# One pair instead of two by owner products, and the first tile's expert rows added by TensorE

## Chip, cores, metric

The kernel runs on one core of one Trainium2 chip. The time is device microseconds of one execution, and the median of several runs is what is compared. Engines: TensorE (PE; PEld is its weight load), VectorE (DVE), ScalarE (ACT), GpSimd (POOL), SyncE (SP); a small q behind a name (SPq) is that engine's own sequencer, which issues transfers.

## What is computed

One encoder layer on x (512 tokens, 1024 columns, float32): a token mixer (windowed attention beside gated linear attention) is added to x, then a mixture of experts, then a last RMS norm. The change touches only what comes after the mixer:

```python
def hier_moe(x, ...):          # top-1 group of 4, then top-2 of the group's 8 experts
    ...
    for gi in range(N_GROUPS):
        h = jax.nn.silu(jnp.einsum('td,edf->tef', xt, w_gate[gi])) * jnp.einsum('td,edf->tef', xt, w_up[gi])
        out = out + jnp.einsum('tef,efd->td', h * combine[:, gi, :, None], w_down[gi])
...
    x = x + hier_moe(hn, ...)
return rms_norm(x, norm_final)
```

There are 32 experts of width 256, and each token goes to two of them. The weights of all experts are 100.7 MB (32 x 3 x 1.05 MB), read once.

## The kernel before

**Pairs.** The experts are worked through two at a time, 16 pairs. A pair has 128 slots, 64 of each of its experts. For pair n the kernel gathers the normed rows of its tokens from DRAM (`gather`, an indirect transfer by GpSimd, 128 x 1024), turns them (`turn_x`: 8 transposes, and copies of the two halves to `xgT` by ScalarE and VectorE), multiplies by the gate and the up weights (`gate_or_up`: 32 products of 256 columns each), takes silu and the product (`h_silu`, `h_sb`), turns the result (`turn_h`, `hT`), and multiplies by the down weights (`down`: 16 products of 512 columns). ScalarE and VectorE scale the two halves of the result by the slot's weight into one buffer `y`, and `scatter` writes its rows to `z_dram` (`expert_rows`). That array has two rows for each token, one for each of its two experts, and was zeroed early.

**Weights.** Each pair has six parts of 1 MB: gate, up and down of two experts. SyncE loads them into a ring of 23 places in the order `order`, each as soon as what lay there is used (`used`). Up to pair 12 the order is up n, gate n+1, down n; for pairs 13 and 14 it is up, down, and then the next gate. TensorE's program has the same order: gate n+1 stands ahead of down n as long as n+1 < LAST.

**The last two pairs.** `LAST` is 14: the loop with gathers, `y` and scatters does pairs 0 to 13. Behind it stands a block `If` for experts with more than 64 tokens, which is skipped with these inputs, and then pairs 14 and 15 are done in another way. Their down result is kept in two float32r parts, high (`ylast[i][0]`, ScalarE) and low (`ylast[i][1]`, VectorE), and TensorE multiplies them by `owner`, a matrix of ones that says which token owns which slot (`to_tokens`, two products of 512 columns a call). This adds the pair's result to the four tiles of 128 tokens without DRAM. A pair takes eight calls (four tiles, two halves of the columns). Pair 15's rows are gathered into a buffer of its own, `xg_last`.

**Where the tiles are summed.** The residual `x2` of tiles 0 and 1 is in SBUF, that of tile 3 in PSUM as `last_rows` (banks 6, 7), and ScalarE copies that of tile 2 to PSUM as `mid_rows` (banks 4, 5) when the last down result has left it (`mid_in`). So for tiles 2 and 3 TensorE adds in place; for tiles 0 and 1 it fills banks 0 to 3 and VectorE adds them to `x2` (`accumulate`, each signalled by `comb_done`, answered by `f_acc`).

**The scattered rows.** When the scatters of pairs 0 to 13 have landed, GpSimd signals `moe_done`, and SyncE loads the 2 MB x 2 of `z_dram` in four transfers of 1 MB (`zt`, one for each tile), with the gain `gfin` of the last norm between the third and the fourth. Tile 0's rows are added by VectorE (`add_row`, twice). Those of tiles 1 to 3 are added by TensorE: `rows_to_tokens` multiplies by `two_rows`, which sums each token's two rows, two float32 products of 512 columns a call, one call for each half of the columns.

**The finish.** For each tile ScalarE sums the squares and forms the mean, GpSimd takes the power -0.5, VectorE scales by it and the gain (tile 3 in two halves), and SyncE stores.

TensorE's order behind the loop, from line 1357 on: turn x of 14, gate and up 14, turn x of 15, turn h of 14, down 14, three calls of `to_tokens`, gate and up 15, three calls, turn h of 15, two calls, down 15, then the last eight calls of `to_tokens` among which stand the two calls of `rows_to_tokens` for tile 1, and at the end those for tile 2 and tile 3.

## Time and profile before

| | us |
|---|---|
| median of 3 runs | 604.86 (603.69 to 605.69) |
| the profiled execution, its time | 605.26 |
| its span, first to last instruction | 603.5 |
| TensorE busy | 577.0 (96% of the span) |
| VectorE, ScalarE, GpSimd busy | 260.3, 215.0, 60.3 |
| mean granted TensorE clock | 0.999 of full speed |
| moved by DMA | 155.78 MB, mean 258 GB/s |

Busy times are shares of the whole span, and this span has stages with different limits; the chain of waits says for each stretch which engine or transfer released the next step, and the windows what each engine did in it. A DMA's "to landing" counts from the start of its issue.

### The profile page before, as it was taken

The page shows a single profiled execution, that of the slowest core. Times are in us where ns is not written, and L with a number is a line of the kernel's source. Part 1 is how long each engine was busy: PE and PEld are TensorE (multiplying, and loading weights), DVE is VectorE, ACT ScalarE, POOL GpSimd, SP SyncE. Part 2 cuts the span into 40 slices and gives each one's busy share as a digit, 9 for nine tenths or more (in the row PEclk, how much of TensorE's full clock was granted, in tenths as well). Part 3 has the DMA queues.
Part 4 walks back from the last instruction along what each step waited for, and adds up shares of the span by engine and source line. Part 5 has one row for each costly group of instructions (what it writes and reads, how often), then busy time and mean ns, then how long its engine had stood idle before and what let it go on. Part 6 is the DMA issues. An engine that isn't in the chain of part 4 may idle for free.

```text
span 603.5 us, 8714 instructions
## 1 busy us (share of the span) xinstructions
PE 577.0 (96%) x3442; PEld 437.3 (72%) x3445; DVE 260.3 (43%) x584; ACT 215.0 (36%) x437; POOL 60.3 (10%) x104
## 2 busy tenths in 40 slices
PE   7999999999999999999999998999999999887795
PEld 4978989888788888888888874766666666543452
DVE  4646677645445765533472375212111211103255
ACT  6634566555786522422152241011111111111114
POOL 3110000001000001100000012012211121112001
PEclk9999999999999999999999999999999999999999
DMA  8365130712231222197789677999999999999995
GB/s 296 92 205 177 59 111 5 287 62 71 71 104 46 61 70 71 38 344 280 287 315 406 248 259 273 389 414 423 424 421 423 424 427 419 424 425 424 424 421 208
DMA packets 59291, 155.78 MB, mean 258 GB/s; under 512 B 8284, under 2 KB 38388, under 8 KB 47600
## 3 DMA queue, kind: packets, MB, share of 16 engines
q1 hardware_dynamic: 54512, 145.74, 63.2%
q0 software_dynamic: 4720, 9.45, 4.1%
q8 instruction: 28, 0.46, 0.3%
q14 instruction: 15, 0.12, 0.1%
q10 hardware_dynamic: 16, 0.00, 0.0%
HBM read 147.31 MB, written 15.75 MB: 270 GB/s over the span
## 4 chain that ended last, share of the span: by engine, by line
PE 79%; DMA 11%; DVE 3%; SPq 3%; ACT 1%; issue 1%; POOL 1%; DVEq 0%; POOLq 0%; ACTq 0%
PE mid_rows L810 17%; PE last_rows L810 16%; PE bank L1247 12%; DMA slot2b<-expert_w_up 9%; PE bank L810 7%; PE bank L803 5%; PE mid_rows L1267 5%; SPq L554 3%; PE bank L1321 2%; PE mid_rows L945 2%; PE last_rows L868 2%; PE mid_rows L1340 1%; DMA w<-w_in 1%; PE bank L1347 1%; PE mid_rows L868 1%; PE bank L923 1%
## 5 line engine op out<-in xcount | busy, mean ns | idle before, releaser
L1247 PE MATMUL bank<-slots,xgT 128*64 128x256 f32 x544 | 73.0, 381 | 4.5 <-DMA slot2b<-expert_w_up 1.9
L1910 DVE TENSOR_TENSOR w_low<-w,w_high 128x1024 fp32r<-128x1024 f32 x32 | 39.2, 1225 | 78.6 <-ACT w_high L1524 78.6
L1247 PEld LDWEIGHTS bank<-slots,xgT 128*64 128x64 f32 x544 | 49.2, 137 | 22.2 <-issue 4.0
L1524 ACT ACTIVATE w_high<-w 128x1024 fp32r<-128x1024 f32 x32 | 33.7, 1054 | 48.6 <-PE last_rows L810 48.6
L2265 DVE TENSOR_SCALAR y<-mid_rows,slot_weights 128x512 f32<-128x512 f32 x14 | 10.5, 751 | 88.4 <-PE mid_rows L1267 88.4
L1699 ACT ACTIVATE y<-mid_rows,slot_weights 128x512 f32<-128x512 f32 x14 | 9.6, 687 | 84.5 <-PE mid_rows L1267 56.4
L1247 PE MATMUL bank<-slot2b,xgT 128*64 128x256 f32 x208 | 32.9, 381 | 0.0
L1267 PE MATMUL mid_rows<-slots,hT 128*64 128x512 f32 x112 | 29.1, 594 | 2.7 <-issue 2.7
L1693 ACT ACTIVATE h_silu<-bank 128x256 f32<-128x256 f32 x14 | 5.4, 384 | 66.3 <-PE bank L1247 66.3
L810 PE MATMUL mid_rows<-x_high,w_high 128*128 128x512 f32 x72 | 28.7, 399 | 0.0
L810 PE MATMUL mid_rows<-x_high,w_low 128*128 128x512 f32 x72 | 28.2, 391 | 0.0
L810 PE MATMUL mid_rows<-x_low,w_high 128*128 128x512 f32 x72 | 28.1, 390 | 0.0
L2255 DVE TENSOR_TENSOR h_sb<-h_silu,bank 128x256 f32<-128x256 f32 x14 | 5.9, 422 | 48.7 <-ACT h_silu L1693 48.7
L1880 DVE CUSTOM_DVE_ANT_0 s_sb<-bank,bias,sink 128x256 f32<-128x256 f32 (+1 forms) x32 | 17.6, 549 | 19.4 <-PE bank L924 19.3
L810 PE MATMUL last_rows<-x_high,w_high 128*128 128x512 f32 x64 | 25.6, 400 | 0.0
L1247 PEld LDWEIGHTS bank<-slot2b,xgT 128*64 128x64 f32 x208 | 21.5, 137 | 5.2 <-issue 1.6
L810 PE MATMUL last_rows<-x_high,w_low 128*128 128x512 f32 x64 | 25.0, 390 | 0.0
L810 PE MATMUL last_rows<-x_low,w_high 128*128 128x512 f32 x64 | 24.9, 390 | 0.0
L1267 PEld LDWEIGHTS mid_rows<-slots,hT 128*64 128x64 f32 x112 | 10.2, 137 | 14.8 <-issue 14.4
L803 PEld LDWEIGHTS bank<-fixed,xg 128*128 128x128 f32 x120 | 14.6, 195 | 7.5 <-issue 5.8
L1503 ACT ACTIVATE softmax<-sink,softmax 128x1 f32<-128x1 f32 x32 | 9.3, 292 | 27.8 <-issue 16.3
L803 PE MATMUL bank<-fixed,xg 128*128 128x128 f32 x120 | 17.4, 288 | 1.2 <-DMA xg<-hn_rows,gtab 1.2
(430 smaller groups left out, 1391.5 us busy)
## 6 DMA issues: line engine op xcount, KB each, us to landing
slots<-expert_w_up SPq DMA_DIRECT2D x18, 1024.0 KB, 23.9
slots<-expert_w_gate SPq DMA_DIRECT2D x17, 1024.0 KB, 12.4
slots<-expert_w_down SPq DMA_DIRECT2D x15, 1024.0 KB, 23.9
slot2b<-expert_w_gate SPq DMA_DIRECT2D x9, 1024.0 KB, 16.9
w<-w_in SPq DMA_DIRECT2D x16, 512.0 KB, 3.6
slot2b<-expert_w_up SPq DMA_DIRECT2D x8, 1024.0 KB, 27.5
slot2a<-expert_w_down SPq DMA_DIRECT2D x6, 1024.0 KB, 21.4
w<-w_in SPq DMA_DIRECT2D x7, 840.0 KB, 4.5
```

The source lines that it names most:

```text
L554: sp.dma_start(ring[q % R], (g_rows, u_rows, d_rows)[m][:, 2 * pair + e, :]).then_inc(m_in[pair % 4][m], 16)
L803: return nc.tensor.transpose(out_, in_, K["ident"][0:n, 0:n])
L810: ins_ = mm(out_, stat[a_], mov[b_], start=first and q_ == 0, stop=last and q_ == 2)
L868: ins = mm(bank[5 + t % 2][:, 0:GW], x_[:, c, t * P:(t + 1) * P], job_view(w_, 0)[:, c, :], start=(h == 0 and q_ == 0 and c == 0), stop=(h ...
L945: ins = mm(bank[4][kv * DH:(kv + 1) * DH, :], tok[:, j, V_AT + kv * DH:V_AT + (kv + 1) * DH], pT[:, kv, k, :], start=(k == 0), stop=(k == ...
L1247: ins = mm(bank[2][e * SLOTS:(e + 1) * SLOTS, m * FE:(m + 1) * FE], xgT[:, c, e * SLOTS:(e + 1) * SLOTS], weights(own, m, e, c * FE, (c + ...
L1267: ins = mm(bank[4 + f][e * SLOTS:(e + 1) * SLOTS, :], hT[:, j, e * SLOTS:(e + 1) * SLOTS], down_rows(own, e, j, f), start=(j == 0), stop=( ...
L1321: ins = mm(bank[2][e * SLOTS:(e + 1) * SLOTS, m * FE:(m + 1) * FE], xgT[:, c, e * SLOTS:(e + 1) * SLOTS], weights(own, m, e, c * FE, (c + ...
L1524: A(wh2[:, u % 2, :], raw2[:, u % 2, :], ACT.Copy).then_inc(s["hi_done"], 1)
L1880: V.tensor_tensor_reduce(s_sb[:, i % 2, 0:n], bank[i % 2][:, 0:n], bias[:, h, band], 1.0, sink[:, h:h + 1], ALU.add, ALU.max, mx[:, i % 2: ...
L1910: V.tensor_tensor(wl2[:, u % 2, :], raw2[:, u % 2, :], wh2[:, u % 2, :].bitcast(F32), ALU.subtract).then_inc(s["lo_done"], 1)
L2265: V.tensor_scalar(y_sb[:, 512:1024], bank[5][:, :], weight, None, ALU.mult).then_inc(s["y_outD"], 1)
```

## The change

- `LAST` becomes 15. Pair 14 goes through the general loop: evaluated into `y`, scattered to `z_dram`, its owner matrix and its eight calls of `to_tokens` gone. Gate 14 moves ahead of down 13, in TensorE's program and in the order of the loads. Pair 15's rows are gathered into the common buffer `xg_in` after the turn of pair 14, and the buffer `xg_last` with its memset and wait is gone; so turn x of pair 15 comes behind down 14.
- SyncE waits for the scatters itself (by `scattered0` and `scattered1`), after `moe_done`, which GpSimd now gives when the last scatter is issued. The gain is loaded ahead of the four `zt` transfers, when down 14 is done. All four have the same layout.
- Tile 0's rows are added by two calls of `rows_to_tokens`, and `add_row` is gone. TensorE's order behind the last down: `to_tokens` for tiles 0, 1, 3 of both halves, rows of tile 0, rows of tile 1, `to_tokens` for tile 2, rows of tile 2, rows of tile 3.
- Tile 3's squares are taken in two halves, each scaled beforehand by the root of 1/1024, the second not before the last product; GpSimd adds the second sum to the first before the power.

The diff, without the parts that only drop the index of the pair:

```diff
-LAST = PAIRS - 2
+LAST = PAIRS - 1
...
-        xg_in, xg_extra, xg_last = (place_at(a_, n_, D)[:, :] for a_, n_ in
-                                    ((XL + D, "xg"), (MG, "xg_extra"), (YA + WSLOT + (NT - 1) * 2 * D, "xg_last")))
+        assert all(arrived[PAIRS - 3, m_] == 128 for m_ in range(3)) and (PAIRS - 3) % 4 == 1
+        xg_in, xg_extra = (place_at(a_, n_, D)[:, :] for a_, n_ in ((XL + D, "xg"), (MG, "xg_extra")))
...
-        ylast = [[place_at(MG + (2 * i_ + j_) * D, f"ylast{i_}{j_}", D, F32R)[:, :] for j_ in range(2)] for i_ in range(2)]
+        ylast = [place_at(MG + j_ * D, f"ylast{j_}", D, F32R)[:, :] for j_ in range(2)]
...
-        owner = v3(place_at(spare, "owner", 2 * SEQ, F32R), SEQ)
-        two_rows = place_at(spare + 2 * SEQ, "two_rows", P // 2)[:, :]
...
+        owner = place_at(spare, "owner", SEQ, F32R)
+        two_rows = place_at(spare + SEQ, "two_rows", P // 2)[:, :]
...
-                if later >= LAST - 1 and (m, e) == (2, 0):
+                if later >= LAST - 2 and (m, e) == (2, 0):
                     used(2, later - 4)
...
+            used(2, LAST - 1)
+            sp.dma_start(gfin, norm_final.partition_broadcast(P)).then_inc(s["gain_in"], 16)
             sp.wait_ge(s["moe_done"], 1)
+            for k in range(2):
+                sp.wait_ge(s[f"scattered{k}"], 16 * ((LAST + 1 - k) // 2))
             for t in range(NT):
                 rows = z_dram[2 * P * t:2 * P * (t + 1), :]
-                if t == NT - 1:
-                    sp.wait_ge(s["lx_done"], 4)
-                    sp.dma_start(gfin, norm_final.partition_broadcast(P)).then_inc(s["gain_in"], 16)
-                sp.dma_start(zt[:, t], rows.rearrange("(p w) n -> p w n", w=2) if t == 0 else
-                             rows.rearrange("(i p) n -> p i n", i=2)).then_inc(s[f"rows_in{t}"], 16)
+                sp.dma_start(zt[:, t], rows.rearrange("(i p) n -> p i n", i=2)).then_inc(s[f"rows_in{t}"], 16)
...
             for n in range(LAST):
-                if n + 2 < PAIRS - 1:
+                if n + 2 < PAIRS:
                     gather(n + 2, n + 2, n % 2, True)
-                else:
-                    pool.wait_ge(s["dn_done"], 2 * (LAST - 1))
-                    nc.gpsimd.memset(xg_last, 0.0).then_inc(s["zeroed"], 1)
-                    pool.wait_ge(s["zeroed"], 9)
-                    gather(PAIRS - 1, PAIRS - 1, 1, False, xg_last)
                 scatter(n, n, n % 2)
-
-            for k in range(2):
-                pool.wait_ge(s[f"scattered{k}"], 16 * (LAST // 2))
...
                 pool.wait_ge(s["ssA_done"], 2 * NT + t + 1)
+                if t == NT - 1:
+                    pool.wait_ge(s["ssA_done"], 3 * NT + 1)
+                    nc.gpsimd.tensor_tensor(rstd3[:, t:t + 1], rstd3[:, t:t + 1], ss2[:, t:t + 1], ALU.add).then_inc(s["last_mean"], 1)
+                    pool.wait_ge(s["last_mean"], 1)
                 nc.gpsimd.tensor_tensor(rstd3[:, t:t + 1], rstd3[:, t:t + 1], half[:, 0:1], ALU.pow).then_inc(s["rstd_done"], 1)
...
-            def to_tokens(i, f, tt, at, first):
-                pe.wait_ge(s["ly_lo"], 2 * i + f + 1)
+            def to_tokens(f, tt, at, first):
+                pe.wait_ge(s["ly_lo"], f + 1)
                 for q_ in range(2):
-                    ins = mm(bank[at][:, :], owner[:, i, tt * P:(tt + 1) * P],
-                             ylast[i][q_][:, f * 512:(f + 1) * 512], start=(first and q_ == 0), stop=(q_ == 1), skip_group_check=True)
+                    ins = mm(bank[at][:, :], owner[:, tt * P:(tt + 1) * P],
+                             ylast[q_][:, f * 512:(f + 1) * 512], start=(first and q_ == 0), stop=(q_ == 1), skip_group_check=True)
                 return ins
...
-            last_turn(0)
-            last_gate_up(0, 0)
-            last_gate_up(0, 1)
-            last_turn(1)
-            last_turn_h(0)
-            last_down(0)
-            pe.wait_ge(s["ltab_done"], NT)
-            to_tokens(0, 0, 0, 0, True).then_inc(s["comb_done"], 1)
-            to_tokens(0, 0, 1, 1, True).then_inc(s["comb_done"], 1)
-            to_tokens(0, 0, 3, 6, False)
-            last_gate_up(1, 0)
-            last_gate_up(1, 1)
-            pe.wait_ge(s["f_acc"], 1)
-            to_tokens(0, 0, 2, 0, True).then_inc(s["comb_done"], 1)
-            pe.wait_ge(s["f_acc"], 2)
-            to_tokens(0, 1, 0, 1, True).then_inc(s["comb_done"], 1)
-            to_tokens(0, 1, 3, 7, False)
-            last_turn_h(1)
-            pe.wait_ge(s["f_acc"], 3)
-            to_tokens(0, 1, 1, 0, True).then_inc(s["comb_done"], 1)
-            pe.wait_ge(s["f_acc"], 4)
-            to_tokens(0, 1, 2, 1, True).then_inc(s["comb_done"], 1)
-            last_down(1)
-            pe.wait_ge(s["ltab_done"], 2 * NT + 1)
-            to_tokens(1, 0, 0, 2, True).then_inc(s["comb_done"], 1)
-            to_tokens(1, 0, 1, 3, True)
-            to_tokens(1, 0, 3, 6, False)
-            pe.wait_ge(s["mid_in"], 1)
-            to_tokens(1, 0, 2, 4, False)
+            last_turn()
+            last_gate_up(0)
+            last_gate_up(1)
+            last_turn_h()
+            last_down()
+            pe.wait_ge(s["ltab_done"], NT + 1)
+            to_tokens(0, 0, 2, True)
+            to_tokens(0, 1, 3, True)
+            to_tokens(0, 3, 6, False)
+            to_tokens(1, 0, 1, True)
+            to_tokens(1, 1, 0, True)
+            to_tokens(1, 3, 7, False)
+            pe.wait_ge(s["rows_in0"], 32)
+            rows_to_tokens(0, 0, 2).then_inc(s["comb_done"], 1)
+            rows_to_tokens(0, 1, 1).then_inc(s["comb_done"], 1)
             pe.wait_ge(s["rows_in1"], 32)
             rows_to_tokens(1, 0, 3).then_inc(s["comb_done"], 1)
-            pe.wait_ge(s["f_acc"], 6)
-            to_tokens(1, 1, 0, 1, True).then_inc(s["comb_done"], 1)
-            to_tokens(1, 1, 1, 0, True)
-            to_tokens(1, 1, 3, 7, False)
             rows_to_tokens(1, 1, 0).then_inc(s["comb_done"], 1)
-            pe.wait_ge(s["mid_in"], 2)
-            to_tokens(1, 1, 2, 5, False)
+            for f in range(2):
+                pe.wait_ge(s["mid_in"], f + 1)
+                to_tokens(f, 2, 4 + f, False)
             for tt, banks in ((2, (4, 5)), (3, (6, 7))):
                 pe.wait_ge(s[f"rows_in{tt}"], 32)
                 for f in range(2):
...
-            for t in range(NT):
+            for t in range(NT - 1):
                 if t < 2:
-                    act.wait_ge(s["f_acc"], 9 + t)
+                    act.wait_ge(s["f_acc"], 2 * (t + 1))
                 else:
-                    act.wait_ge(s["comb_done"], (12, 14)[t - 2])
+                    act.wait_ge(s["comb_done"], 2 * (t + 1))
                 if t >= 1:
                     act.wait_ge(s["ssA_done"], 2 * NT + t)
                 act.wait_ge(s["act_step"], step(A(junk3[:, :], summed_rows(t), ACT.Square, accum_out=ss3[:, t:t + 1])))
                 A(rstd3[:, t:t + 1], ss3[:, t:t + 1], ACT.Copy, scale=1.0 / D, bias=EPS).then_inc(s["ssA_done"], 1)
+            t = NT - 1
+            act.wait_ge(s["ssA_done"], 2 * NT + t)
+            act.wait_ge(s["comb_done"], 2 * NT - 1)
+            act.wait_ge(s["act_step"], step(A(junk3[:, 0:512], last_rows[:, 0:512], ACT.Square, accum_out=ss3[:, t:t + 1], scale=ROOT)))
+            A(rstd3[:, t:t + 1], ss3[:, t:t + 1], ACT.Copy, bias=EPS).then_inc(s["ssA_done"], 1)
+            act.wait_ge(s["comb_done"], 2 * NT)
+            A(junk3[:, 512:D], last_rows[:, 512:D], ACT.Square, accum_out=ss2[:, t:t + 1], scale=ROOT).then_inc(s["ssA_done"], 1)
...
-            def add_row(i):
-                return step(V.tensor_tensor(x2[:, 0, :], x2[:, 0, :], zt[:, 0, i, :], ALU.add))
...
-            dve.wait_ge(s["rows_in0"], 32)
-            dve.wait_ge(s["f_acc"], 6)
-            first_row = add_row(0)
-            last_low(1, 0)
-            dve.wait_ge(s["dve_step"], first_row)
-            second_row = add_row(1)
-            last_low(1, 1)
-            dve.wait_ge(s["dve_step"], second_row)
-            accumulate(7, 0, 0, 2)
-            accumulate(8, 1, 0, 3)
-            accumulate(9, 0, 1, 1)
-            accumulate(10, 1, 1, 0)
+            last_low(0)
+            last_low(1)
+            accumulate(1, 0, 0, 2)
+            accumulate(2, 0, 1, 1)
+            accumulate(3, 1, 0, 3)
+            accumulate(4, 1, 1, 0)
```

## Rows read from the trace of the kernel before

**Rows 1.** Page, slices of the span (GB/s in each 40th) and GpSimd's DMA queue.
```profile
GB/s 296 92 205 177 59 111 5 287 62 71 71 104 46 61 70 71 38 344 280 287 315 406 248 259 273 389 414 423 424 421 423 424 427 419 424 425 424 424 421 208
...
q0 software_dynamic: 4720, 9.45, 4.1%
```

**Rows 2.** Chain of waits, 555 to 604 us: start, us, what.
```profile
532.32 30.16 DMA slot2b<-expert_w_up
...
562.62 3.67 PE bank L1321 x32
...
583.80 3.58 PE mid_rows L1340 x16
...
589.44 1.01 PE bank L1353 x4
...
593.71 1.89 PE mid_rows L1353 x8
```

**Rows 3.** Windows: length, then PE, PEld, DVE, ACT, POOL busy, PEclk, DMA, GB/s.
```profile
562.62:587.38 24.76, 24.00 (x157) 13.94 (x157) 9.49 (x16) 3.43 (x6) 0.00 (x0) 1.00 1.01 422
587.38:597.29 9.91, 9.91 (x41) 4.12 (x40) 6.79 (x8) 5.80 (x12) 1.37 (x3) 1.00 0.47 195
```

**Rows 4.** Line 745's scatters (all 14); line 664's loads, the last one alone.
```profile
L745 POOL DMA_INDIRECT expert_rows<-y,zcol x14: 1002/1011/1023, 395.3 to 555.9; - x14
...
DMA to landing us min/median/max: 7.8/8.1/9.0
...
L664 SPq DMA_DIRECT2D zt<-expert_rows x1: 4573/4573/4573, 570.8 to 570.8; - x1
...
DMA to landing us min/median/max: 22.4/22.4/22.4
```

**Rows 5.** Timeline of TensorE, 548.4 to 563 us: start, us, instruction, idle before.
```profile
549.43 0.50 PE L803 MATMUL bank<-fixed,h_sb 128*128 128x128 f32 x2 [0.94 <-DVE h_sb L2255]
550.45 3.65 PE L1267 MATMUL mid_rows<-slot2a,hT 128*64 128x512 f32 x16 [0.52 <-DVE hT L2259]
554.04 1.16 PE L803 MATMUL bank<-fixed,xg 128*128 128x128 f32 x8
556.03 4.33 PE L1321 MATMUL bank<-slot2b,xgT 128*64 128x256 f32 x32 [0.83 <-DVE xgT L2326]
```

**Rows 6.** Timeline of TensorE's weight loads within line 1321's first 32 products.
```profile
556.03 0.62 PEld L1321 LDWEIGHTS bank<-slot2b,xgT 128*64 128x64 f32 x7 [1.02 <-DVE xgT L2326]
557.18 2.72 PEld L1321 LDWEIGHTS bank<-slot2b,xgT 128*64 128x64 f32 x25 [0.52 <-issue]
```

**Rows 7.** Line 554: last loads of the up and of the down weights.
```profile
L554 SPq DMA_DIRECT2D slots<-expert_w_up x1: 2339/2339/2339, 552.2 to 552.2; - x1
...
DMA to landing us min/median/max: 24.9/24.9/24.9
...
L554 SPq DMA_DIRECT2D slots<-expert_w_down x1: 2264/2264/2264, 558.0 to 558.0; - x1
...
DMA to landing us min/median/max: 24.0/24.0/24.0
```

**Rows 8.** Timeline of ScalarE and GpSimd: a half copy, tile 2's squares, two one-column operations.
```profile
588.02 0.59 ACT L1755 ACTIVATE mid_rows<-x 128x512 f32<-128x512 f32 x1
...
595.62 1.03 ACT L1763 ACTIVATE squares<-mid_rows 128x1024 f32<-128x1024 f32 x1 [0.42 <-PE mid_rows L1353]
...
596.77 0.20 ACT L1764 ACTIVATE row_norms<-row_norms 128x1 f32<-128x1 f32 x1
...
5.63 0.19 POOL L685 TENSOR_SCALAR row_norms<-row_norms 128x1 f32<-128x1 f32 x1 [3.43 <-ACT squares L1414]
...
598.79 0.55 POOL L794 TENSOR_TENSOR row_norms<-row_norms,half 128x1 f32<-128x1 f32 x1 [1.20 <-ACT row_norms L1764]
```

**Rows 9.** Timeline of TensorE at the start: products of zeros.
```profile
1.80 2.74 PE L830 MATMUL last_rows<-nil_rows 128*128 128x512 bf16 x6 [1.80 <-POOL nil_rows L680]
...
8.24 1.03 PE L830 MATMUL last_rows<-nil_rows 128*128 128x512 bf16 x4
```

123 lines of the change are left out of this document (46 added, 77 removed).

## Prediction

> **What bounds the kernel now.** I read four views, in this order. The page's slices come first: DMA moves 421 to 425 GB/s from the 26th slice to the 39th, so from about 380 us almost to the end the transfers are saturated [rows 1]. The chain of waits then says where that stops mattering. The up weights of pair 14 are on their way for 30.16 us and land at 562.48; from there the chain is TensorE work: up of pair 14 at 562.62, the last down from 583.80, a call of `rows_to_tokens` for 1.01 (four records, two per float32 product), and two calls for tile 2 in 1.89 [rows 2]. So there is a front part that ends when bytes have landed, and a back part that TensorE sets. The windows split the back part in two: from the start of up 14 to the end of the last down, 562.62 to 587.38, TensorE is busy 24.00 of 24.76 us; from there to 597.29 it is busy all 9.91 us, with 40 weight loads, that is 0.248 us for each product [rows 3]. After 597.29 come squares on ScalarE, a power on GpSimd, the scaling on VectorE and the store, to 603.5.
>
> I therefore sum the change in four terms: when up 14 can start, how long from there to the end of the last down, how many products follow, and how long the finish is. All are against the profiled execution (605.26 us with a span of 603.5), which is 0.40 above the median of the runs, 604.86; I carry the difference over to the median.
>
> **Term 1, start of up 14.** The new order of loads swaps gate 14 and down 13 and moves no byte, so up 14 stays at the same place in the queue. TensorE now does gate 14 at once after the turn of pair 14 and down 13 behind it; both lie in the time in which it waits for the landing anyway: before, it had 2.26 us of idle ahead of up 14, and down 13 will only wait for its own weights there. One thing moves in the queue: the scatter of pair 13, issued at 555.90 before [rows 4], follows down 13, so it goes out after up 14's weights have landed or nearly. GpSimd's queue moved 9.45 MB [rows 1] in its 30 gathers and scatters, 0.3 MB each, or 0.7 us at 424 GB/s. Bounds: 0 and -0.7; I take **-0.3**, since some of it has not moved by 562.5 either way.
>
> **Term 2, up 14 to the end of the last down.** Removed from TensorE between them: eight calls of `to_tokens` for pair 14 (16 products at 0.248, 4.0 us). But they covered other things, which now stand bare. Three stalls, each priced by what pair 13 and the turn of pair 14 show [rows 5]: the end of up to the start of down is 548.49 (549.43 less its idle 0.94) to 550.45, 1.96 us, for silu, product, turn and copy, and it now comes twice; the end of down 13 at 554.10 to the start of the next gate at 556.03 is 1.93 us, for the turn of x and its two copies, which before was hidden for pair 15 under silu of pair 14. Then there is gate 14 itself, 4.33 us where an up of the same 32 products takes 3.67: within it the weight loads stopped for 0.52 at 557.18, with nothing in the profile to wait for [rows 6]. It is the first such block behind the skipped `If`; before, the DMA wait hid it, and now gate 15 is that block, so I charge it. The sum is 3.67 + 1.96 + 3.65 + 1.93 + 4.33 + 3.67 + 1.96 + 3.65 = 24.82, against 24.76 before: **0.0**. Without the stop it would be -0.7.
>
> The landings set a floor under this. The last up weights were issued at 552.2 and took 24.9 us (577.1), the last down weights at 558.0 and took 24.0 (582.0) [rows 7]; the scatters of pairs 13 and 14 now lie in front of the second, up to 0.7 us more. With terms 1 and 2 the last up wants its weights near 577.8 and the last down near 583.4, so both are just covered. The floor for the end of the last down is 582.0 + 3.65 = 585.7, or 586.4 with the scatter. My own is 587.1.
>
> **Term 3, products after the last down.** Before: eight calls of `to_tokens` (16 records) and six of `rows_to_tokens` (24), 9.91 us. After: again eight, but eight of `rows_to_tokens`, as tile 0's two are new, 48 records. Eight more at 0.248 are 2.0; by the 1.89 of tile 2's two calls it is 1.9. I take **+1.9**. What they replace are the two adds of rows on VectorE, which lay beside TensorE's work and were on no chain, so nothing is gained there. TensorE must pass every one of these products, in order, before tile 3 is complete. The wait for the low part of the second half of the columns costs nothing: it is ready about 1.5 us after down, and three calls cover that.
>
> **Term 4, the finish.** Tile 3's squares are halved: the first half runs while the last product call runs, the second behind it. But tile 2's squares come first: they begin when tile 2 is complete, 1.9 us before the end of TensorE, and take 595.62 to 596.97 with the copy of the mean, 1.35 us. A half of 512 columns from the 512-column copy (0.59) plus the read of the sum is about 0.7, its copy 0.2, then 0.7 again [rows 8]: ScalarE ends 1.1 us behind TensorE (before: 1.4). GpSimd gets an add ahead of its power. No row has this add of one column: the nearest are its multiply-add of one column, 0.19, and its power, 0.55 [rows 8]; I take 0.28 with the hand-over, as it is arithmetic like the first. Sum: -0.3 + 0.3 = **0.0**, bounds -0.4 and +0.5.
>
> **What is hidden.** The pair-14 evaluation into `y`, its scatter and the wait for it replace owner work: ScalarE and VectorE are idle there. The order of things for the rows is: down 14 ends near 571.9, y is written to 572.7, the scatter goes out at 573.6 and lands 7.8 to 9.0 us later [rows 4], at 581.4 to 582.6. SP, which has nothing else to do, issues the four loads then. Before, four loads and the gain landed by 593.2; the last load by itself took 22.4 us from its issue at 570.8, behind the weights [rows 4]. After, the queue still holds the last weights and the gain until about 584, so the loads follow without a hole and at 2.5 us each land at about 586.5, 589, 591.5 and 594. TensorE wants them at 590.2, 592.2, 595.3 and 597.2. The cover is 3 us; beyond it each us of lateness is one on the end. One rule of the Trainium skill bears on that cover: the page "DMA: Bandwidth & Descriptors", section "Anatomy of one DMA — SWDGE (gpsimd) path", gives a fixed cost of some 2 us beside the bytes; an estimate by it puts a load of 1 MB on an empty queue at 4.4 us, the first rows at 587, and changes no term.
>
> **Sum.** -0.3 + 0.0 + 1.9 + 0.0 = +1.6 us: 606.9 for the profiled execution, **606.5** for the median. By the low ends it is -1.0 (the floor 586.4) + 1.8 - 0.4 = +0.4, by the high ends 0 + 0.2 + 2.1 + 0.5 = +2.8.
>
> **Rivals.** (a) *The landing floor is reached.* The stop in gate 15 does not come and the last down starts as its weights land: 586.4, and with the cheap finish +0.4 us, 605.3. For it: the stop is seen once. (b) *The rows come late.* The scatter is now on the path of all four loads; if it lands over 3 us later than any in the trace, or the loads run at half their pace, tile 3's rows are last: +1 to +4 us more, 607.5 to 610.5. Against it: 14 scatters landed within 7.8 to 9.0. (c) *The clock falls.* TensorE now idles in one piece, down 13's end (559.5) to up 14, up to 3.0 us, where the longest shown is 2.26 at a granted clock of 1.00. At a lower level up 14 would go at the pace of the first products, 0.46 each against 0.26 of the same kind later [rows 9], by 1.77: 2.8 us on 3.67, so 609.3. The Trainium skill, page "TensorE: Matmul & The Clock Gate", section "HAM oscillation — how this bites in real kernels", states such a fall after a DMA wait between bursts; by that rule it would be 609.3 too, while the trace keeps its clock over every gap it has. (d) *Faster.* The 4.0 us of pair 14's products come off whole, because silu, turn and copies overlap with something: the last down ends at 583.4, the tail adds 1.9, -2.1 us, 602.8. It decides only if the last down weights have landed by 579.7; they landed at 582.0, and I see no bytes that leave the queue.
>
> **Chances.** Measurements of this kernel tell about 0.3% from no change, 1.8 us, and my sum lies just inside. The forecast 0.60, (a) 0.15, (b) 0.12, (c) 0.06, (d) with anything unseen 0.07. The forecast's own range is 605.6 to 607.7, and I put 0.4 of it beyond 606.7. Slower: 0.12 + 0.06 + 0.24 = 0.42; faster 0.07; the same 0.51. The range from 604.6 to 609.0 holds the forecast, (a) and most of (b), and leaves (d) and most of (c) out.
>
> **What would show it.** Up 14 starts at 562 to 562.6; the last down starts without a DMA wait, or with one if (a); from its end to the last product 11.8 us with 48 weight loads and no idle; all `zt` loads issued at 581 to 583 and landed by 595; a gap of 0.5 in the weight loads of gate 15; granted clock 1.00 throughout; ScalarE's last sum 1.1 us behind TensorE. It is wrong if the end of the last down is not within 586.3 to 587.6, or if TensorE waits for rows.

## The result, and the profile after

| | before | after |
|---|---|---|
| median of the runs taken together on one chip | 605.28 us (603.69 to 606.94, 20 runs) | 606.14 us (605.55 to 607.14, 20 runs) |
| the profiled execution, its time | 605.26 | 605.96 |
| its span | 603.5 | 604.2 |
| TensorE busy | 577.0 | 577.9 |
| moved by DMA | 155.78 MB | 156.02 MB |

The ratio is 1.0014 with an interval of 1.0007 to 1.002: the changed kernel is slower by about 0.9 us, and that is within the 0.3% (1.8 us) that the prediction counts as no change. In the profiled executions it is slower by 0.7.

Read first the page of the changed kernel: the engines' busy time, the row of GB/s in 40 slices, GpSimd's queue, and the shares of the chain.

```profile
PE 577.9 (96%) x3436; PEld 436.3 (72%) x3437; DVE 252.6 (42%) x570; ACT 214.5 (36%) x438; POOL 61.2 (10%) x106
...
GB/s 300 87 206 177 57 113 3 294 55 71 71 104 54 53 69 71 42 341 289 289 314 400 241 271 274 386 416 421 425 421 423 423 426 421 425 424 425 423 369 257
...
q0 software_dynamic: 4864, 9.69, 4.2%
...
PE 77%; DMA 11%; SPq 5%; DVE 3%; ACT 2%; issue 1%; POOL 1%; DVEq 0%; POOLq 0%; ACTq 0%
```

The queue is as saturated as before up to the 38th slice [rows 1]; then 369 and 257 stand where 421 and 208 stood, because the rows are now loaded at the very end. GpSimd's queue moved 0.24 MB more, the pair that is scattered now.

Then the chain of waits of the changed kernel, from 540 us on: start, length, what.

```profile
551.83 25.35 DMA slots<-expert_w_up
577.18 0.14 issue
577.31 3.69 PE bank L1320 x32
...
582.94 3.65 PE mid_rows L1338 x16
586.59 1.12 PE bank L1345 x4
...
589.84 3.58 PE bank L1351 x16
593.42 1.13 PE mid_rows L1345 x4
594.55 1.89 PE mid_rows L1351 x8
```

This differs from [rows 2] in one thing that matters. Before, the last transfer in the chain was the up weights of pair 14, landing at 562.48. Now it is the up weights of pair 15, landing at 577.18. In this chain all that TensorE does between them is off the path.

The windows of the changed kernel, cut at the same three events as [rows 3] (start of up 14, end of the last down, last product), with the finish as the third:

```profile
562.00:586.59 24.59, 20.43 (x141) 10.85 (x141) 5.67 (x15) 2.74 (x5) 2.17 (x3) 1.00 0.98 396
586.59:598.14 11.55, 11.54 (x49) 4.82 (x48) 6.08 (x7) 6.10 (x13) 1.84 (x3) 1.00 0.68 270
598.14:604.20 6.06, 0.00 (x0) 0.00 (x0) 2.69 (x3) 1.17 (x5) 1.04 (x3) 0.75 0.69 277
```

In the first, TensorE is busy 20.43 of 24.59 us, where it was busy 24.00 of 24.76: 3.6 us of work went and only 0.17 of time. In the second it is busy throughout, as before, with 48 weight loads instead of 40. The four terms of the prediction, against the profiled execution of before (span +0.7):

| term | forecast | measured | from |
|---|---|---|---|
| 1. start of up 14 | -0.3 | -0.62 | 562.62 to 562.00 |
| 2. up 14 to the end of the last down | 0.0 | -0.17 | 24.76 to 24.59 |
| 3. products behind it | +1.9 | +1.64 | 9.91 to 11.55 |
| 4. finish | 0.0 | -0.15 | 603.5 - 597.29 = 6.21, to 6.06 |
| sum | +1.6 | +0.70 | |

TensorE's timeline of the changed kernel shows where the stalls lie, and one thing that was not expected (below): start, length, instruction, idle before it.

```profile
556.28 5.35 PE L1266 MATMUL mid_rows<-slot2b,hT 128*64 128x512 f32 x16 [2.47 <-issue]
562.00 3.24 PE L1246 MATMUL bank<-slot2b,xgT 128*64 128x256 f32 x28 [0.37 <-DMA slot2b<-expert_w_up]
...
577.31 3.67 PE L1320 MATMUL bank<-slots,xgT 128*64 128x256 f32 x32 [0.41 <-DMA slots<-expert_w_up]
581.92 0.50 PE L802 MATMUL bank<-fixed,h_sb 128*128 128x128 f32 x2 [0.93 <-DVE h_sb L2307]
582.94 3.65 PE L1338 MATMUL mid_rows<-slots,hT 128*64 128x512 f32 x16 [0.52 <-DVE hT L2309]
```

The line 1266 row is down of pair 13. Its 16 products took 5.35 us; the last down takes 3.65, as it did before. The windows over it show why (the column behind the five busy times is the granted clock):

```profile
556.20:556.70 0.50, 0.42 (x2) 0.23 (x4) 0.00 (x0) 0.00 (x0) 0.00 (x0) 1.00 1.00 418
556.70:557.20 0.50, 0.50 (x4) 0.19 (x2) 0.00 (x0) 0.00 (x0) 0.00 (x0) 0.65 0.98 410
557.20:560.00 2.80, 2.80 (x8) 0.90 (x6) 0.00 (x0) 0.51 (x1) 0.00 (x0) 0.50 1.03 430
560.00:560.40 0.40, 0.40 (x4) 0.29 (x2) 0.00 (x0) 0.18 (x1) 0.16 (x1) 0.67 0.97 410
560.40:561.60 1.20, 1.20 (x6) 0.17 (x2) 0.00 (x0) 0.00 (x0) 0.02 (x1) 1.00 1.03 430
```

TensorE had idled 2.47 us (the view says "issue", but the last down weights of pair 13 landed only at 556.19), began at full clock, fell to 0.50 (the 1.2 GHz level) some 0.6 us later, and had it back at about 560.2. Down 13 ended at 561.63, and up 14 waited another 0.37 us for its weights: the fall was hidden, with that to spare.

Last, the four loads of the rows in the changed kernel:

```profile
L666 SPq DMA_DIRECT2D zt<-expert_rows x4: 377/466/1163, 580.8 to 582.9; - x4
...
DMA to landing us min/median/max: 5.7/8.8/11.6
```

They were issued at 580.77, 581.2, 582.4 and 582.9 and landed at 586.5, 589.3, 592.0 and 594.5; TensorE wanted them at 589.8, 591.6, 594.5 and 596.2. It waited for none, with 1.8 to 3.3 us to spare.

### The profile page after: what moved, and what is told of

It reads as the page before. It is cut to its first block, busy times and chain, and to the rows that moved or that the text cites. A ratio compares the mean times of both kernels' runs of the same rounds, so it can differ in the third digit from the quotient of the medians.

```text
span 604.2 us, 8686 instructions
## 1 busy us (share of the span) xinstructions
PE 577.9 (96%) x3436; PEld 436.3 (72%) x3437; DVE 252.6 (42%) x570; ACT 214.5 (36%) x438; POOL 61.2 (10%) x106
## 2 busy tenths in 40 slices
DMA packets 59563, 156.02 MB, mean 258 GB/s; under 512 B 8368, under 2 KB 38472, under 8 KB 48000
## 4 chain that ended last, share of the span: by engine, by line
PE 77%; DMA 11%; SPq 5%; DVE 3%; ACT 2%; issue 1%; POOL 1%; DVEq 0%; POOLq 0%; ACTq 0%
PE mid_rows L809 17%; PE last_rows L809 16%; PE bank L1246 12%; DMA slots<-expert_w_up 9%; PE bank L809 7%; PE bank L802 5%; SPq L555 5%; PE mid_rows L1266 5%; PE mid_rows L944 2%; PE last_rows L867 2%; DMA w<-w_in 1%; PE mid_rows L867 1%; PE bank L922 1%; PE bank L1117 1%; PE bank L923 1%
## 5 line engine op out<-in xcount | busy, mean ns | idle before, releaser
L1246 PE MATMUL bank<-slot2b,xgT 128*64 128x256 f32 x240 | 36.6, 381 | 0.4 <-DMA slot2b<-expert_w_up 0.4
L1246 PEld LDWEIGHTS bank<-slot2b,xgT 128*64 128x64 f32 x240 | 23.6, 137 | 7.5 <-DMA slot2b<-expert_w_up 1.2
## 6 DMA issues: line engine op xcount, KB each, us to landing
slots<-expert_w_down SPq DMA_DIRECT2D x15, 1024.0 KB, 24.8
```

What stands on the lines that cost most here:

```text
L1246: ins = mm(bank[2][e * SLOTS:(e + 1) * SLOTS, m * FE:(m + 1) * FE], xgT[:, c, e * SLOTS:(e + 1) * SLOTS], weights(own, m, e, c * FE, (c + ...
```

## The experiments

Eleven runs, ten of them of a kernel with something altered and one of the changed kernel again, in three batches, each timed against runs of the kernel before on the same chip. By the numbers in their names, the first batch is `e1`, `e2`, `e3` and `e5`, the second `e4`, `e8`, `e9` and `after_again`, the third `e6`, `e7` and `e11`. The medians of before were 605.63 (31 runs), 605.19 (24 runs) and 605.46 (24 runs); in the second batch the changed kernel was run again (`after_again`):

> The changed kernel itself, on the same chip as the three above, so that they can be set against it: 0.14% above the kernel before, by either theory. Its granted clock in down 13 shows whether the fall there comes each time.

Measured: 606.40 (11 runs), ratio 1.0021, interval 1.0012 to 1.003, which agrees with the first result; its down 13 took 5.35 us as well, and its up 14 started at 561.90. Medians of one kernel differ by up to 0.44 us between batches (605.19 to 605.63), so smaller differences are not read from times of different batches; there the ratios to the kernel before are compared. Where a rise or fall inside a kernel is told, it is from its profiled execution, and spans are compared (before 603.5, changed 604.2, changed again 604.1).

**Rows of tile 0 by TensorE, in the kernel before (`e2_before_rows0_tensor`).** The third term alone.

```diff
...
             to_tokens(1, 0, 0, 2, True)
+            pe.wait_ge(s["rows_in0"], 32)
+            rows_to_tokens(0, 0, 2).then_inc(s["comb_done"], 1)
...
             to_tokens(1, 1, 0, 1, True)
+            rows_to_tokens(0, 1, 1).then_inc(s["comb_done"], 1)
...
-            first_row = add_row(0)
...
-            second_row = add_row(1)
```

> The kernel before with only this part of the change: tile 0's rows are added by TensorE with two calls behind the last down, and not by VectorE. My theory: eight more product records on the path, +1.7 to +1.9 us, near 607.1. Rival (the calls hide in waits of the tail or run faster among others): under +0.8.

Measured: 607.38 (8 runs) against 605.63, ratio 1.0027, interval 1.0014 to 1.0039, span 605.5, +2.0. So the eight records do cost, and VectorE's two adds, now gone, give nothing that shows. The chain of waits of this kernel behind its last down shows the price of each call:

```profile
587.76 1.01 PE bank L1352 x4
588.77 0.67 PE bank L1346 x2
589.43 0.46 PE last_rows L1346 x2
...
595.83 1.89 PE mid_rows L1352 x8
```

A pair of products costs 0.46 where the same kind stands ahead of it and 0.67 right behind a call of `rows_to_tokens`. From the first product here (587.06) to the end of the last (597.53 + 1.89 = 599.42) it is 12.36 us, and by the same reading of before's trace it was 9.96: +2.4 for the eight records in before's order. In the changed kernel the rows of tiles 0 and 1 stand together, 16 records in 3.58 us or 0.224 each, and the term was +1.64. So the new order of calls gives back about 0.8 us of what the new products cost. Here the last down ended 0.3 earlier than in before's trace, so the span rose by 2.0 and not by 2.4.

**Rows of tile 0 by VectorE, in the changed kernel (`e1_rows0_vector`).** The reverse.

```diff
...
-            pe.wait_ge(s["rows_in0"], 32)
-            rows_to_tokens(0, 0, 2).then_inc(s["comb_done"], 1)
-            rows_to_tokens(0, 1, 1).then_inc(s["comb_done"], 1)
...
             last_low(0)
             last_low(1)
+            dve.wait_ge(s["rows_in0"], 32)
+            dve.wait_ge(s["dve_step"], add_row(0))
+            dve.wait_ge(s["dve_step"], add_row(1))
```

> The changed kernel with one part undone: tile 0's rows are added by VectorE again, here behind the two low parts (so from about 588.1), and TensorE has six calls for rows. My theory (the tail of products sets the end, 16 records of rows cost 3.58 us, half of that is tile 0's): the last product ends 1.8 us sooner, near 596.4, and the time is about 1.7 us under the changed kernel, near 604.4, which is also under the kernel before. Rival (VectorE becomes the bound: its two adds of 1.2 us delay tile 0's and tile 1's sums, and with them ScalarE's squares): less than 0.8 us gained.

Measured: 606.51 (12 runs, 605.03 to 607.22), ratio 1.0007, interval 0.9996 to 1.0018; the profiled execution was the fastest of them, with a span of 603.3. There the last down ended at 586.69, but TensorE came to tile 1's rows earlier and found them missing:

```profile
590.57 1.94 PE L1352 MATMUL bank<-zt,two_rows 128*64 128x512 f32 x8 [0.64 <-DMA zt<-expert_rows]
592.43 1.20 PE L1346 MATMUL mid_rows<-ylast,owner 128*128 128x512 f32 x4
593.57 1.94 PE L1352 MATMUL mid_rows<-zt,two_rows 128*64 128x512 f32 x8
```

Of the 1.8 us that leave TensorE (eight records at 0.224), 0.64 come back as that wait, and tile 3's rows landed at 595.50 for products that start at 595.54, 0.2 behind the pace of the ones ahead. The last product ends at 597.48, 0.66 sooner than in the changed kernel and not 1.7 as expected. By the spans it is 0.9 below the changed kernel; by the ratios 0.4, with intervals that overlap, so this run alone does not prove the price of the eight records.

**The rows held back (`e4_rows_held`).** To see where their cover ends, SyncE issues the loads only when the first half of the last down is done.

```diff
+            sp.wait_ge(s["ldn_done"], 1)
             for t in range(NT):
                 rows = z_dram[2 * P * t:2 * P * (t + 1), :]
```

> The changed kernel with the four loads of the rows held until the first half of the last down is done (near 584.9 instead of 580.8). By the landings of the changed kernel the rows had 3.3, 2.3, 2.5 and 1.8 us to spare for tiles 0 to 3. My theory (that spare is the cover, and the last landings follow the issue by as much as the queue is empty then): TensorE waits for rows and the time rises by 1 to 2.4 us. Rival (the loads are paced by other transfers ahead, so the hold costs nothing): the same within 0.3 us.

Measured: 607.39 (5 runs), ratio 1.0035, interval 1.0021 to 1.0048, so 1.0 above the changed kernel in the same batch (with only five runs, and intervals that overlap). The loads left at 584.9 to 586.3, that is 3.4 to 4.1 us later, and landed in 4.8 to 10.9. Waits on `zt` now stand ahead of tile 1's rows (0.51, 592.19), and tile 3's start at 597.28, 1.0 later than in the changed kernel. With 1.8 to 3.3 us of cover and 3.4 to 4.1 of delay, about one microsecond should show, and one did.

**Tile 3's squares whole again (`e3_whole_squares`).** The fourth term.

```diff
-            for t in range(NT - 1):
+            for t in range(NT):
...
-                if t == NT - 1:
-                    pool.wait_ge(s["ssA_done"], 3 * NT + 1)
-                    nc.gpsimd.tensor_tensor(rstd3[:, t:t + 1], rstd3[:, t:t + 1], ss2[:, t:t + 1], ALU.add).then_inc(s["last_mean"], 1)
-                    pool.wait_ge(s["last_mean"], 1)
...
```

> The changed kernel with tile 3's squares taken whole again and no add on GpSimd. By the two traces the way from the last product to tile 3's scaling took 2.21 us with halves and 2.08 whole, so my theory expects the same time within 0.2 us, rather a little less. Rival (the halves hide part of the squares and save 0.4 us or more): 0.4 to 0.6 us more than the changed kernel.

Measured: 606.65 (11 runs), ratio 1.0018, interval 1.0006 to 1.003, span 604.1. The changed kernel's ratio is 1.0014 to 1.0021: no difference that can be told, as the term's 0.0 said.

**Gate 14 behind down 13 again (`e8_old_order`).** TensorE's order and that of the loads as before.

```diff
-            turns += ([(n_, 1), (n_ + 1, 0), (n_, 2)] if n_ + 1 < LAST else
+            turns += ([(n_, 1), (n_ + 1, 0), (n_, 2)] if n_ + 1 < LAST - 1 else
...
-                if n + 1 < LAST:
+                if n + 1 < LAST - 1:
                     gate_or_up(n + 1, 0, *weights_of(n + 1))
...
                 down(n, *weights_of(n))
+                if n + 1 == LAST - 1:
+                    gate_or_up(n + 1, 0, *weights_of(n + 1))
```

> The changed kernel with down 13 ahead of gate 14 again, in TensorE's program and in the order of the loads. Theory A (the swap only moves work about in the time in which TensorE waits for up 14's weights): the same as the changed kernel within 0.3 us, up 14 between 561.8 and 562.5. Theory B (the swap itself brings the fall of the clock in down 13 and costs in the median): no fall between 550 and 562, and 0.4 us or more less.

Measured: 606.95 (8 runs), ratio 1.003, interval 1.0019 to 1.004; 0.55 above the changed kernel of the batch, with intervals that overlap. Timeline of its TensorE:

```profile
557.07 5.13 PE L1246 MATMUL bank<-slot2b,xgT 128*64 128x256 f32 x32 [2.49 <-DMA slot2b<-expert_w_gate]
563.37 1.51 PE L1246 MATMUL bank<-slot2b,xgT 128*64 128x256 f32 x11 [1.16 <-DMA slot2b<-expert_w_up]
```

Now gate 14 waits for its weights for 2.49 us and takes 5.13 us instead of 3.67, and up 14 starts 1.37 later than in the changed kernel, waiting for weights that are themselves late. Its scatter of pair 13 went out at 556.38, ahead of those weights' landing, against 563.42 in the changed kernel. By itself this fits the reason given for term 1; but 0.3 MB is 0.7 us at 424 GB/s and the start moved by 1.37, so the scatter is at most half of it. Part of the rest was there before the orders differ: the first load in another order is issued at 518.81, and the up weights that land at 525.53 and 528.00 in the changed kernel, issued long before, landed at 525.87 and 528.84 here. And `e2_before_rows0_tensor`, which has before's order and sends that scatter at 556.64, also ahead of the landing, starts up 14 at 561.78, earlier than the changed kernel. So executions of one order differ here by as much as the two orders do, and the scatter's share isn't shown.

**TensorE kept busy in the gap (`e5_kept_busy`).** Nine products of constants that nobody reads, between gate 14 and down 13 (eight of them are in the trace's records).

```diff
+                if n == LAST - 2:
+                    keep_busy(9)
                 down(n, *weights_of(n))
```

> The changed kernel with nine products of constants (bfloat16, 512 columns, into a free bank) between gate 14 and down 13, where TensorE idled 2.47 us before its clock was granted at 0.50 within down 13. Theory A (the fall is hidden in the wait for up 14's weights): down 13 takes 3.65 instead of 5.35 us, the granted clock stays at 1.00, up 14 still starts at 562.0 and the time is the same within 0.2 us. Theory B (in the median run the fall reaches up 14 or delays the scatter of pair 13 so that later steps are late): 0.3 to 0.8 us less.

Measured: 606.86 (12 runs: eight from 606.43 to 606.90, four from 608.41 to 608.64), ratio 1.0024, interval 1.0012 to 1.0036. Its timeline, and its windows over up 14 (which begins at 561.77):

```profile
553.60 1.89 PE L1117 MATMUL bank<-fixed,onesb 128*128 128x512 bf16 x8 [0.16 <-issue]
556.05 3.65 PE L1266 MATMUL mid_rows<-slot2b,hT 128*64 128x512 f32 x16 [0.56 <-issue]
561.77 1.08 PE L1246 MATMUL bank<-slot2b,xgT 128*64 128x256 f32 x8 [2.07 <-DMA slot2b<-expert_w_up]
```

```profile
562.60:563.00 0.40, 0.40 (x8) 0.26 (x6) 0.00 (x0) 0.00 (x0) 0.00 (x0) 1.00 1.07 451
563.00:566.00 3.00, 3.00 (x18) 1.76 (x16) 0.00 (x0) 0.00 (x0) 0.00 (x0) 0.51 1.01 425
566.00:566.60 0.60, 0.60 (x6) 0.31 (x4) 0.00 (x0) 0.00 (x0) 0.00 (x0) 0.61 0.97 403
```

Down 13 has its 3.65 back, and ends 2.07 us before the weights of up 14 land. Behind that gap the clock falls again, in up 14, which took 5.36 us instead of 3.67. Gate 15 started at 574.68, 1.46 later than in the changed kernel, and the last down at 583.77, 0.83 later. In this execution, filling a covered gap opened a bare one. The median rose too, but by the ratios only by 0.2 to 0.6 us over the changed kernel, with intervals that overlap. What puts four of the runs 1.6 us above the others isn't shown; each profile is one execution.

**Less to load (`e6_before_less_bytes`, `e7_less_bytes`).** Half the columns of the second up part of pair 13 are not loaded, 0.52 MB, in the kernel before and in the changed one. Half of one expert's up weights are left out of the computation.

```diff
+                if later == PAIRS - 3 and order[q][1:] == (1, 1):
+                    sp.dma_start(ring[q % R][:, 0:PART // 2], u_rows[:, 2 * later + 1, 0:PART // 2]).then_inc(m_in[later % 4][1], 16)
+                    continue
                 load_part(q)
```

> The kernel before, with half the columns of the second up part of pair 13 not loaded: 0.52 MB leave the queue ahead of the up weights of pair 14, 1.24 us at 424 GB/s. It leaves out half of one expert's up weights, so that expert's result is formed with what lay in the place. Theory (the front part ends when bytes have landed, the back part is TensorE's): up of pair 14 starts 1.2 us earlier, at 561.4, and all behind it too, so the time falls by 1.2 us, unless down 13 and gate 14 hold it at their own pace (end of gate 14 at 560.4, so not before that). Rival (the transfers are not what sets the front): no change of the median beyond 0.3 us.

> The changed kernel with the same half of the second up part of pair 13 not loaded (it leaves out half of one expert's up weights). Theory: up of pair 14 is allowed by its weights at 560.8 instead of 562.0, but down 13 with its clock fall (556.3 to 561.6) now ends behind that, so it starts at 561.6 to 561.7, only 0.4 us earlier; the last down's weights land 1.2 us earlier too and gate 15 to the last down keep their pace, so the median falls by 0.4 us, the 0.41 of waiting ahead of the last up goes as well: 0.4 to 0.8 us in all. Rival (the fall of the clock does not come, or is no limit): 1.2 us less, as for the kernel before.

Measured: the kernel before went to 603.60 (6 runs), ratio 0.9969, interval 0.9958 to 0.9981, span 601.8, -1.7. The changed one went to 605.37 (11 runs, 604.25 to 607.54), ratio 1.0004, interval 0.9991 to 1.0016, with 604.25 and a span of 602.5 in the profiled execution, -1.7 too. The kernel before moved by more than the 1.24 us of the bytes. The changed one did so in its profiled execution, which is the fastest of its eleven; by the ratios it fell by 0.6 to 1.0 us only, its runs spread over 3.3 us, and that is about what the theory (0.4 to 0.8) had put. The theory's mechanism, that down 13 with its fall of the clock would hold the start of up 14 back, is refuted by the profile all the same: down 13 itself started earlier, at 554.54, fell likewise (5.35 us), and up 14 began at 560.19, 1.81 sooner. The chains of waits of the two, first `e6_before_less_bytes`, then `e7_less_bytes`:

```profile
549.93 25.53 DMA slots<-expert_w_up
...
575.60 3.67 PE bank L1324 x32
```

```profile
549.97 25.48 DMA slots<-expert_w_up
...
575.58 3.69 PE bank L1323 x32
```

In both the last up starts 0.14 us behind the landing of its weights (575.46 and 575.45), and all behind it moved with that, 1.7 us. This is the answer to where the removed work went: the kernel before and the changed one have the same floor there. In before the last up started at 577.27 with the weights landed at 577.13 [rows 7]; its row in the timeline shows no idle,

```profile
577.27 3.67 PE L1321 MATMUL bank<-slots,xgT 128*64 128x256 f32 x32
```

and in the changed kernel it started at 577.31, with a landing of 577.18. The weight loads tell more than the products. First before's, then the changed kernel's first load of the last up:

```profile
577.24 0.88 PEld L1321 LDWEIGHTS bank<-slots,xgT 128*64 128x64 f32 x10 [0.35 <-issue]
```

```profile
577.28 0.84 PEld L1320 LDWEIGHTS bank<-slots,xgT 128*64 128x64 f32 x9 [0.84 <-issue]
```

Both come 0.10 to 0.11 us behind the landing, and the one of before behind a pause of 0.35 where the pauses inside a block are under 0.1. So before, too, started its last up on the landing: its loads waited some 0.3 us, while its products, still busy with the ones ahead, show no idle. After, the products idle 0.41 there. In `e2_before_rows0_tensor`, which has before's front, the last up waited 0.45 us for its weights. Of the eight calls of pair 14 three lay ahead of this landing, where nothing is gained, and five between the last up and the last down, where silu, product, turn and copy take 1.96 us without them. What was gained lies there: from the start of the last up to the end of the last down it took 10.11 us before (577.27 to 587.38) and 9.28 after (577.31 to 586.59).

Why 0.52 MB were worth 1.7 us and not 1.24 in the two profiles has a likely answer in them. The up weights that landed at 475.11 in before and at 475.12 in the changed kernel landed at 474.54 and 474.53 here, 40 us ahead of the issue of the shortened load. These two executions were thus 0.6 us early before the edit could act, and without that 1.1 is left in each, near the 1.24. What gave them the head start isn't shown.

The traces with before's front also bear on the stop of 0.52 in gate 14, which the prediction priced. In `e6_before_less_bytes` the weight loads of gate 14 stop for 0.15, in `e2_before_rows0_tensor` not at all:

```profile
557.19 2.73 PEld L1324 LDWEIGHTS bank<-slot2b,xgT 128*64 128x64 f32 x25 [0.15 <-issue]
```

```profile
556.71 3.22 PEld L1320 LDWEIGHTS bank<-slot2b,xgT 128*64 128x64 f32 x32 [1.83 <-DVE xgT L2328]
```

The block began at 556.03 in before, at 556.42 and at 556.71 here, and the stop ended at 557.18 in before [rows 6] and at 557.19 in `e6_before_less_bytes`: the later the start, the shorter the stop. So it looks like a wait for something that came at about 557.2 and not like a fixed cost; what came then isn't shown.

**A tail without its two new costs (`e9_vector_rows_reordered`).** In the changed kernel: tile 0's rows by VectorE, tile 3's squares whole, and tile 2's owner products ahead of tile 1's rows, which gives these 1 us more to land.

```diff
...
+            for f in range(2):
+                pe.wait_ge(s["mid_in"], f + 1)
+                to_tokens(f, 2, 4 + f, False)
             pe.wait_ge(s["rows_in1"], 32)
             rows_to_tokens(1, 0, 3).then_inc(s["comb_done"], 1)
             rows_to_tokens(1, 1, 0).then_inc(s["comb_done"], 1)
-            for f in range(2):
-                pe.wait_ge(s["mid_in"], f + 1)
-                to_tokens(f, 2, 4 + f, False)
...
```

> The changed kernel with tile 0's rows on VectorE (as in the first experiment), tile 3's squares whole, and TensorE's two owner calls for tile 2 ahead of the rows of tile 1. The first experiment ended its products at 597.48, after 0.64 us of waiting for tile 1's rows (landed at 590.52). My theory (with that wait filled by work that is ready, the tail is the bare count of products): last product near 596.5, a span near 602.8, 1.4 us under the changed kernel and 0.6 us under the kernel before. Rival (the rows' landings are now the bound and only move the wait to tile 2 or 3): last product at 597.4 as in the first experiment.

Measured: 605.15 (11 runs), ratio 1.0000, interval 0.9991 to 1.001: 1.25 below the changed kernel of the same batch, clear of its interval (1.0012 to 1.003), and level with before. Tile 1's rows are not waited for now; the wait went to tile 3's:

```profile
591.01 1.94 PE L1348 MATMUL bank<-zt,two_rows 128*64 128x512 f32 x8
592.78 1.93 PE L1348 MATMUL mid_rows<-zt,two_rows 128*64 128x512 f32 x8
595.68 1.94 PE L1348 MATMUL last_rows<-zt,two_rows 128*64 128x512 f32 x8 [0.97 <-DMA zt<-expert_rows]
```

The last of the rows were issued at 583.5 and took 12.2 us, to 595.7. So the landing of the rows is the next bound: of the 1.8 us of products taken away, the wait of 0.97 keeps half.

**The gain behind the rows (`e11_gain_behind`).** As the last, with the gain's load moved behind the four of the rows.

```diff
-            sp.dma_start(gfin, norm_final.partition_broadcast(P)).then_inc(s["gain_in"], 16)
...
                              rows.rearrange("(i p) n -> p i n", i=2)).then_inc(s[f"rows_in{t}"], 16)
+            sp.dma_start(gfin, norm_final.partition_broadcast(P)).then_inc(s["gain_in"], 16)
```

> As e9_vector_rows_reordered, with the gain of the last norm (0.5 MB written to 128 partitions) issued behind the four loads of rows instead of ahead of the scatter of pair 14. Theory (the rows' landings bind there): rows land up to 1.2 us earlier, the wait of 0.97 ahead of tile 3's rows goes, the last product ends at 596.7; but the gain lands last, near 595.0, and VectorE's four scalings of 1.3 us each stand behind it, so tile 3's starts near 598.9 against 599.7: the median is 0.6 to 0.8 us below e9's. Rival (the rows' landings are not moved by the gain's bytes, as these went out ten microseconds earlier): the wait stays at 1 us, and the late gain costs 0.5 us or so instead.

Measured: 606.26 (12 runs), ratio 1.0012, interval 1.0 to 1.0023, span 603.7: not below the last, but some 0.7 us above it by the ratios (the intervals overlap) and 0.2 by the spans. TensorE and VectorE in its timeline:

```profile
594.39 1.94 PE L1348 MATMUL last_rows<-zt,two_rows 128*64 128x512 f32 x8 [0.28 <-DMA zt<-expert_rows]
```

```profile
595.59 2.48 DVE L2312 SCALAR_TENSOR_TENSOR x<-x,row_norms,gfin 128x1024 f32<-128x1024 f32 x2 [2.46 <-DMA gfin<-norm_final]
597.98 1.28 DVE L2312 SCALAR_TENSOR_TENSOR x<-mid_rows,row_norms,gfin 128x1024 f32<-128x1024 f32 x1
599.18 1.40 DVE L2312 SCALAR_TENSOR_TENSOR x<-last_rows,row_norms,gfin 128x512 f32<-128x512 f32 x2
```

The rows did land 1.3 earlier and the last products start 1.29 earlier, as the theory had it; its price for the late gain was too low. VectorE waited 2.46 us for it, to 595.59, and its four scalings then stand end to end up to tile 3's, which starts only 0.50 sooner (599.68 to 599.18), and all stores leave late together behind it. What puts four of the twelve runs above 607 isn't shown.

## Why the prediction was nearly right, step by step

The forecast was 606.5 with its own range of 605.6 to 607.7; 606.14 came. Part of that nearness is luck. The forecast stood on 604.86, the median of three runs, and the median of 20 is 605.28; from there the same sum would have said 606.9. Set against before, the sum was +1.6, and +0.7 was seen in the profile, +0.86 in the medians: the change costs about half of what was forecast. In the profile's terms rival (a), with its +0.4, is nearer than the forecast.

- **Term 3 is what the change costs, and it was named.** Measured +1.64 for +1.9, 48 weight loads, no idle, 11.55 us for 11.8. The mechanism is confirmed from one side by `e2_before_rows0_tensor` (+2.0 in the span). From the other, `e1_rows0_vector` gave back only 0.66 us of products, as a wait for rows took the rest, and `e9_vector_rows_reordered`, which alters three things at once, gave back 1.25 in the median. It was sized as eight times the mean of before's tail; the grouping of calls, worth some 0.8 us, was not seen, nor that the products in question cost 0.3 each in before's order.
- **Term 2's pieces held, its stop did not.** From the start of up 14 to that of gate 15 the pieces make 3.67 + 1.96 + 3.65 + 1.93 = 11.21; measured 11.22 (562.00 to 573.22). The last up to the end of the last down was put at 3.67 + 1.96 + 3.65 = 9.28, and took 9.28. But the 0.66 charged for a stop in the weight loads of gate 15 did not come: its loads follow each other without a gap. Nor is the stop a price of the first block behind the skipped `If`, as the prediction had it. It behaves like a wait for something that comes at about 557.2 (the two rows of weight loads in the section on less to load). In place of the stop stood 0.41 of waiting for the last up's weights, which makes 11.22 + 3.67 + 0.41 + 9.28 = 24.58. This is the step that failed: "so I charge it", from one stop seen once. Rival (a), which had the stop away and the last down ending on a landing at 586.4, largely came true (586.59), but by the up weights, not the down weights; those landed at 582.7 with 0.2 to spare.
- **Term 1 came out at twice its size, and its reason isn't shown**: up 14 started 0.62 earlier, not 0.3, near the bound of 0.7. But with before's order it started at 562.62, 561.78 (`e2_before_rows0_tensor`) and 563.37 (`e8_old_order`), so the 0.62 lies within what executions of one order differ by. Since the last up waits for its own landing, this moved nothing behind it: with up 14 at 562.3 the wait would have been 0.1 and the rest the same.
- **Term 4**: -0.15 for 0.0, and taking it back changes nothing that can be measured. GpSimd's add took 0.19, as the nearest row said; ScalarE's last sum ended at 599.34, 1.2 behind TensorE (forecast 1.1).
- **The rows (rival (b))** were covered: issued at 580.8 to 582.9, landed by 594.5, as forecast (581 to 583, "about 586.5, 589, 591.5 and 594"). The cover, put at 3 us, was 1.8 to 3.3. They are the next bound, though: take the new products away and TensorE waits for them. The estimate of 4.4 us for a load of 1 MB on an empty queue rests on a figure for transfers that GpSimd issues, and SyncE issues these. The only such load here, the first of `e4_rows_held`, took 4.8 (nothing was moved from 584 to 585, and it left at 584.88); in the changed kernel the first took 5.7.
- **The clock (rival (c))**: "granted clock 1.00 throughout" was wrong. The fall came one block ahead of the named place, in down 13, and cost 1.70 us there (5.35 for 3.65) that nobody waited for. In `e5_kept_busy`, where it came at up 14, it cost 1.69 on the block, not the 2.8 that were taken from the first products. The Trainium skill, page "TensorE: Matmul & The Clock Gate", section "HAM oscillation — how this bites in real kernels", describes a slow spell at the start of each burst behind a DMA wait of some 3 to 5 us; the traces agree in kind, but here such spells came behind gaps of 2.07 and 2.47 us (and of 2.03 elsewhere, below), shorter than the waits it tells of.
- **Faster (rival (d))** needed last down weights by 579.7; they came at 582.7, and the last up's own at 577.18 forbade it already. The prediction looked for the floor at the down weights and gave the up weights "just covered", which they were, to 0.4 us on the wrong side. The kernel before stood on that landing already, as its weight loads show.
- **A reading**: the slices of [rows 1] stand at 389 and 414 in the 26th and 27th and at 419 to 427 from the 28th to the 38th, so the transfers are saturated from about 407 us and not from 380. Nothing in the sum hangs on it.

Three things stay open: why the executions of one altered kernel spread in some experiments over 2 to 3 us, where the profiled one was often near the fastest; what the stop of 0.52 in before's gate 14 waited for; and why the start of up 14 differs by up to 1.6 us between executions with the same order.

## What to carry to other kernels

When weights stream at the full rate of the queue, work removed from an engine between two landings gives nothing but the little by which the engine was late for the second; look up the landing behind the removed work before you price the work, and look for it in the weight loads as well as in the products, which can hide a short wait. What is moved to the far side of the last landing, onto the one engine that sets the end, counts in full, however idle the other engines are. Calls of one kind set side by side are cheaper than the same calls interleaved, and filling a gap that costs nothing may open one that does. Before a single pause is priced as a fixed cost, look at a second execution in which the block starts at another time.

## What the runs showed of the hardware that was not expected

- **TensorE's clock fell behind gaps of 2.03 to 3.29 us, and not behind every one.** At down 13 it fell behind 2.47 us of idle in the changed kernel and behind 2.08 to 3.29 in seven other executions with the same order (2.08 in `e3_whole_squares`, 3.25 in `e7_less_bytes`, 3.29 in `e4_rows_held`); in `e5_kept_busy` behind 2.07 at up 14, in `e8_old_order` behind 2.49 at gate 14. The kernel before had a gap of 2.26 ahead of up 14 and kept 1.00. The gap of about 2.05 some 16 us earlier (2.05 ahead of 540.18 in the changed kernel) was passed at 1.00 there, in before, in `e8_old_order` and in `e9_vector_rows_reordered`, and the clock fell behind it in `e1_rows0_vector` (2.04, at 540.14), `e4_rows_held` (2.03, at 539.44), `e11_gain_behind` and in `e2_before_rows0_tensor` and `e6_before_less_bytes`, which have before's front. The changed kernel taken again also fell at 529.33, where the first execution did not. So the length of the last gap alone doesn't tell, and the same code keeps the clock in one execution and loses it in another. The granted clock went to 0.50, the 1.2 GHz level, in `e8_old_order` already within the gap (0.83 on average from 556 to 557, where nothing ran, and 0.50 from 557.07), in the changed kernel only when work had gone on for 0.6 us. What a block loses by it was 1.40 (down 13 in `e9_vector_rows_reordered`, 5.05), 1.46 (gate 14 in `e8_old_order`), 1.69 (up 14 in `e5_kept_busy`) and 1.70 us (5.35 for 3.65, down 13 in six kernels).
- **A pair of owner products (float32r) costs 0.46 us behind its like and 0.67 behind products of the rows (float32)**; those cost 0.25 a record in groups of four and 0.224 in a group of 16.
- **A load of 1 MB took 4.8 to 6.1 us from issue to landing with nothing, or only the rest of the last weights and the gain, ahead of it on the queue, and 24 to 31 on the full queue.** The first load of rows took 4.8 in `e4_rows_held`, 5.7 in the changed kernel and 6.1 in `e1_rows0_vector`; the weights behind 520 us took 24.8 to 30.9 in the changed kernel.
